# Twelve half quarters of two down projections as seven block products each, in a fused two-block kernel on one core

## The chip, the cores and the metric

One NeuronCore of a Trainium2 chip runs the whole program. The metric is the device time of one execution in microseconds (us); a shorter time is better. TensorE (PE in the profile) multiplies matrices into the eight PSUM banks, VectorE (DVE), ScalarE (ACT) and GpSimd (POOL) work on elements, and SyncE (SP) issues transfers.

## The reference

Two transformer blocks run one after the other on 512 tokens of width 1024. Each ends with a feed-forward network, and only these two networks are changed:

```python
hf = _rmsnorm(h, norm_ffn_g[l]) @ w_ff1[l]                # first block, 1024 -> 4096
h = h + jnp.square(jax.nn.relu(hf)) @ w_ff2[l]            # 4096 -> 1024
...
m = rmsnorm(x, norm_pre_mlp[l])                           # second block
y = jnp.square(jax.nn.relu(m @ w_up[l])) @ w_down[l]
x = x + rmsnorm(y, norm_post_mlp[l])
```

All is float32. The kernel computes each product from two float32r parts of each operand, the rounded value (`_hi`) and the remainder (`_lo`): hi·hi + hi·lo + lo·hi, three matmuls for one.

## The kernel before

The activations lie by feature: 128 features on the partitions, 512 tokens along the row. The weights come as a stream of chunks of 128x1024 elements (512 KB), in the order of use, through a ring of four buffers. For each chunk SP issues the load into `w_raw` (L386 to L389), ACT rounds it to `w_hi` (`round_chunk`, L1213 to L1218, three chunks ahead), POOL subtracts to give `w_lo` (`remainder`, L408 to L410), and PE does `chunk` (L524): eight blocks of the inner dimension, three matmuls for each (`three`, L511, through `mm`, L509), all into one bank. A chunk is 24 matmuls of 128x128 weights on 512 columns.

A feed-forward network (`feed_forward`, at L826 on PE, L1500 on ACT, L2161 on DVE) is four quarters (`FF_GROUPS = 4`), and a quarter is eight up chunks and then eight down chunks. Behind each up chunk DVE takes relu(bank)·rstd into `ff_t` (L2146), ACT squares it into `ff_f` (L1494) and rounds that to `b_hi` (L1496), and DVE makes `b_lo` (L2149). Behind each down chunk DVE adds the bank to `res` or `ffy` (L2157; L2154 copies it for the first quarter of the second network). The first network is the stage FF1, the second FF2. The first up chunks of each run beside the end of the stage before: in FF1 chunks 0 and 1 take turns block by block while the residual is being split, in FF2 chunks 0 to 2 run by halves of the tokens while POOL and DVE finish the residual (`post_add`, L481 to L485). Each engine takes its instructions in the written order, so a wait on a semaphore holds all that stands behind it on that engine.

Of the kernel before, what the change touches and what calls it, by code (L numbers as in the profile page):

```python
# [20 lines left out]
ALU = mybir.AluOpType  # L21
ACT = mybir.ActivationFunctionType
AX = mybir.AxisListType
F32 = mybir.dt.float32
# [3 lines left out]
P = 128  # L28
# [22 lines left out]
FF_GROUPS = 4  # L51
# [10 lines left out]
          ("GL", 3), ("AO", 8), ("CO", 8), ("MX", 8), ("QX", 4), ("OX", 4), ("FF1", 64), ("CQ", 2), ("CKV", 1),  # L62
          ("KR", 1), ("QK", 4), ("UQ", 2), ("UKV", 1), ("OA", 1), ("VM", 4), ("OM", 3), ("WO", 8), ("FF2", 64)]
CH = {}
_n = 0
for _name, _count in STAGES:
# [5 lines left out]
        ("GL", 3), ("AO", 8), ("CO", 8), ("MX", 8), ("QX", 4), ("OX", 8), ("FF1", 64), ("CQ", 2), ("CKV", 1),  # L72
        ("KR", 1), ("QK", 4), ("UQ", 8), ("UKV", 8), ("OA", 1), ("VM", 4), ("OM", 3), ("WO", 11), ("FF2", 68)]
# [94 lines left out]
def program(nc, stream, xT, memT, cols_in, consts_in, pos_in, out):  # L168
    with ExitStack() as ctx:
# [80 lines left out]
        ff_f = at("ff_f", [P, 2, T], TMP0 + 4096)  # L250
# [68 lines left out]
        x_landed = [sem(f"x_landed{i}") for i in range(RING)]  # L319
# [43 lines left out]
        def up_bank(s, g, o0, j):  # L363

            if s == 1 and g == 0 and j in (4, 5):
                return j + 2
            return (o0 + j) % RING
# [6 lines left out]
        def _(sp):  # L374
# [11 lines left out]
            with sp.Fori(1, CHUNKS // RING) as i:  # L386
                for j in range(RING):
                    sp.wait_ge(chunk_done, RING * i + j - (RING - 1))
                    sp.dma_start(w_raw[:, j, :],  # L389
                                 stream[bass.ds(RING * i + j, 1), :, :].rearrange("o p n -> (o p) n")  # L390
                                 ).then_inc(raw_landed[j], 16)
            vector_adds = [j for j in range(KB) if j not in POOL_ADDS]
# [12 lines left out]
        def _(pool):  # L405
# [6 lines left out]

            last = CH["FF2"] // RING
# [7 lines left out]
            pool.wait_ge(sems["first_hi"], 1)  # L421
            first_remainder(0, sems["first_lo"])
# [3 lines left out]
            with pool.Fori(1, CH["CQ"] // RING) as i:  # L426
                for j in range(RING):
                    remainder(RING * i + j, j)
            pool.wait_ge(sems["pv_done"], 4 * MLA_G)
# [65 lines left out]
            with pool.Fori(last + 1, CHUNKS // RING) as i:  # L495
                for j in range(RING):
                    remainder(RING * i + j, j)
# [9 lines left out]
        def _(pe):  # L507
# [147 lines left out]
            def first_values():  # L655
                for kk in range(2):
                    w = slice(kk * T, (kk + 1) * T)
                    pe.wait_ge(w_hi_done if kk else sems["first_hi"], 1)
# [3 lines left out]
                for kk in range(2):  # L662
                    w = slice(kk * T, (kk + 1) * T)
                    pe.wait_ge(w_lo_done if kk else sems["first_lo"], 1)
# [161 lines left out]
            def feed_forward(name, s, hset, norm, norm_at, upto=2 * KB, done=0):  # L826
                c0, o0 = CH[name], O[name]

                def ff_chunk(g, j, ready=None, base=0, ks=range(KB)):
                    hi, lo = (a_hi, a_lo) if j < KB else (b_hi, b_lo)  # L830
                    if isinstance(g, int) and up_bank(s, g, o0, j) >= RING:
                        chunk(c0 + j, (c0 + j) % RING, None, up_bank(s, g, o0, j), hi, lo)
                        return
                    chunk(g * 16 + (c0 + j), (c0 + j) % RING, g * 16 + (o0 + j), (o0 + j) % RING, hi, lo, T,
                          ready, base, first=o0 + j, ks=ks)

                if not done:
                    for k in range(KB):
                        ff_chunk(0, 0, sems["hg_ready"], KB * hset, range(k, k + 1))
                        ff_chunk(0, 1, ks=range(k, k + 1))  # L840
                    done = 2
                ff_chunk(0, done, ks=range(norm_at))
                norm()
                ff_chunk(0, done, ks=range(norm_at, KB))
                for j in range(done + 1, 2 * KB):
                    ff_chunk(0, j, sems["f_ready"] if j == KB else None, 32 * s)
                with pe.Fori(1, FF_GROUPS - 1) as g:
                    for j in range(2 * KB):
                        ff_chunk(g, j, sems["f_ready"] if j == KB else None, g * KB + 32 * s)
# [1940 lines left out]
```

## Time and profile before

| | |
|---|---|
| time, three runs | 1583.17 us median (1582.39 to 1584.31) |
| profiled execution, first to last instruction | 1579.8 us span |
| PE busy | 1545.0 us, 98% of the span |
| DVE, ACT, POOL busy | 838.6, 652.4, 653.6 us |
| largest share of the chain that ended last | PE, 90% |

The profile is one execution. Its span leaves out what lies before the first and behind the last instruction: 3.4 us to the median of the runs. Matmuls overlap in the pipeline, so the spacing of their starts tells their cost, not the duration of one.

### The profile page before, as it was taken

What the parts mean: (1) busy time and instruction counts of PE and PEld (TensorE: products, weight loads), DVE (VectorE), ACT (ScalarE), POOL (GpSimd) and SP (SyncE); (2) the same over time, 40 slices, a digit from 0 to 9 for tenths busy, and PEclk for the clock granted to TensorE, in tenths of its full rate; (3) what the DMA queues carried; (4) which work ended last, traced back from release to release, by engine and by line L of the source; (5) the groups of instructions that cost most, each with busy time, mean ns of one, the idle gap of its engine ahead of it and who ended that gap; (6) DMA issues with size and microseconds to landing.
All of it is one profiled execution on the core that took longest, in us unless ns stands there. A gap on an engine that the chain in (4) does not pass through costs nothing.

```text
span 1579.8 us, 21097 instructions
## 1 busy us (share of the span) xinstructions
PE 1545.0 (98%) x7370; PEld 1278.8 (81%) x7370; DVE 838.6 (53%) x1486; ACT 652.4 (41%) x1066; POOL 653.6 (41%) x299
## 2 busy tenths in 40 slices
PE   8999999999999999999999999999999999999997
PEld 6888888787788877888888888777778888888887
DVE  5689999877785446442112124877645612111125
ACT  6553333444552445523233244455754514232331
POOL 3454444323344433444444445442524544444442
PEclk9999999999999999999999999999999999999999
DMA  5332333222333322323333333221112333333332
GB/s 208 102 121 94 94 101 98 67 67 67 107 95 102 96 67 67 101 93 99 101 93 93 104 96 94 83 71 61 41 49 73 96 104 93 94 98 102 94 93 81
DMA packets 41412, 144.57 MB, mean 92 GB/s; under 512 B 4596, under 2 KB 6772, under 8 KB 41080
## 3 DMA queue, kind: packets, MB, share of 16 engines
q1 hardware_dynamic: 40320, 139.94, 28.7%
q10 hardware_dynamic: 1016, 3.62, 0.7%
q8 instruction: 48, 0.79, 0.2%
q14 instruction: 28, 0.23, 0.1%
HBM read 141.43 MB, written 2.11 MB: 91 GB/s over the span
## 4 chain that ended last, share of the span: by engine, by line
PE 90%; DVE 4%; issue 3%; ACT 2%; POOL 1%; DMA 0%; DVEq 0%; SPq 0%; POOLq 0%; ACTq 0%
PE bank L509 88%; PE bank L619 1%; POOL w_lo L410 1%; POOL res L485 1%; DVE cq_rstd L1767 0%; PE bank L1014 0%; DVE bias L1913 0%; ACT w_hi L1218 0%; DMA x_raw<-in_xT 0%; DMA w_raw<-in_stream 0%; ACT kT L1392 0%; DVE cn_lo L2261 0%; DVE gt L2284 0%; DVE ffy L2600 0%; ACT probs L1251 0%
## 5 line engine op out<-in xcount | busy, mean ns | idle before, releaser
L410 POOL TENSOR_TENSOR w_lo<-w_raw,w_hi 128x1024 fp32r<-128x1024 f32 x250 | 602.6, 2411 | 849.6 <-ACT w_hi L1218 849.2
L1218 ACT CAST w_hi<-w_raw 128x1024 fp32r<-128x1024 f32 x255 | 267.4, 1049 | 499.2 <-DMA w_raw<-in_stream 499.2
L509 PE MATMUL bank<-a_hi,w_hi 128*128 128x512 f32 (+1 forms) x1120 | 445.0, 397 | 3.1 <-DVE a_lo L2520 1.8
L509 PE MATMUL bank<-a_hi,w_lo 128*128 128x512 f32 (+1 forms) x1120 | 431.5, 385 | 0.0
L509 PE MATMUL bank<-a_lo,w_hi 128*128 128x512 f32 (+1 forms) x1120 | 431.2, 385 | 0.0
L509 PEld LDWEIGHTS bank<-a_hi,w_hi 128*128 128x128 f32 x1120 | 210.5, 188 | 50.9 <-issue 4.2
L509 PEld LDWEIGHTS bank<-a_lo,w_hi 128*128 128x128 f32 x1120 | 210.6, 188 | 45.6 <-issue 3.6
L509 PEld LDWEIGHTS bank<-a_hi,w_lo 128*128 128x128 f32 x1120 | 210.4, 188 | 42.3
L509 PE MATMUL bank<-b_hi,w_hi 128*128 128x512 f32 (+1 forms) x640 | 244.3, 382 | 0.0
L509 PE MATMUL bank<-b_hi,w_lo 128*128 128x512 f32 (+1 forms) x640 | 242.3, 379 | 0.0
L509 PE MATMUL bank<-b_lo,w_hi 128*128 128x512 f32 (+1 forms) x640 | 242.2, 378 | 0.0
L509 PEld LDWEIGHTS bank<-b_hi,w_hi 128*128 128x128 f32 x640 | 120.4, 188 | 22.8 <-issue 0.2
L509 PEld LDWEIGHTS bank<-b_lo,w_hi 128*128 128x128 f32 x640 | 120.4, 188 | 22.5 <-issue 0.2
L509 PEld LDWEIGHTS bank<-b_hi,w_lo 128*128 128x128 f32 x640 | 120.4, 188 | 22.5
L2146 DVE SCALAR_TENSOR_TENSOR ff_t<-bank,rstd 128x512 f32<-128x512 f32 x64 | 44.1, 689 | 148.5 <-PE bank L509 148.4
L2149 DVE TENSOR_TENSOR b_lo<-ff_f,b_hi 128x512 fp32r<-128x512 f32 x64 | 47.9, 748 | 86.8 <-ACT b_hi L1496 86.8
L1977 DVE SCALAR_TENSOR_TENSOR bank<-conv_in,cols,bank 128x512 f32<-128x512 f32 x114 | 82.3, 749 | 1.6
L2157 DVE TENSOR_TENSOR res<-bank,res 128x512 f32<-128x512 f32 x32 | 22.1, 691 | 109.0 <-PE bank L509 109.0
L1956 DVE SCALAR_TENSOR_TENSOR bank<-conv_in,cols,bank 128x512 f32<-128x512 f32 x116 | 76.5, 745 | 0.0
L1494 ACT ACTIVATE ff_f<-ff_t 128x512 f32<-128x512 f32 x64 | 40.5, 632 | 85.5 <-DVE ff_t L2146 85.5
L2157 DVE TENSOR_TENSOR ffy<-bank,ffy 128x512 f32<-128x512 f32 x20 | 13.8, 691 | 84.3 <-PE bank L509 84.3
L1260 ACT COPY probsT<-bank 128x256 f32<-128x256 f32 (+3 forms) x48 | 19.6, 409 | 58.0 <-PE bank L619 58.0
(355 smaller groups left out, 1961.3 us busy)
## 6 DMA issues: line engine op xcount, KB each, us to landing
w_raw<-in_stream SPq DMA_DIRECT2D x255, 512.0 KB, 3.5
res<-in_xT ACTq DMA_DIRECT2D x1, 2048.0 KB, 8.0
out_y<-y_out SPq DMA_DIRECT2D x16, 128.0 KB, 1.8
x_raw<-in_xT SPq DMA_DIRECT2D x3, 512.0 KB, 8.3
mem_raw<-in_memT SPq DMA_DIRECT2D x1, 1024.0 KB, 11.9
mrow<-m_rows ACTq DMA_DIRECT2D x4, 256.0 KB, 3.2
w_raw<-in_stream SPq DMA_DIRECT2D x2, 256.0 KB, 3.6
x_raw<-in_xT SPq DMA_DIRECT2D x2, 256.0 KB, 4.2
```

Of the source, the lines that this page charges most:

```text
L410: nc.gpsimd.tensor_tensor(w_lo[:, j, :], w_raw[:, j, :], w_hi[:, j, :].bitcast(F32), ALU.subtract).then_inc(w_lo_done, 1)
L485: nc.gpsimd.tensor_tensor(res[:, j, t], res[:, j, t], mixed[:, j, t], ALU.add).then_inc(sems["post_added"], 1)
L509: return nc.tensor.matmul(o, l, r, start=start, stop=stop)
L619: m = nc.tensor.transpose(turned_bank(U)[:, r], probs[:, U % 2, r], ident)
L1218: A.copy(w_hi[:, slot, :], w_raw[:, slot, :]).then_inc(w_hi_done, 1)
L1260: A.copy(probsT[:, U % 2, r], turned_bank(U)[:, r]).then_inc(sems["pT_copied"], 1)
L1494: A.activation(ff_f[:, j % 2, :], ff_t[:, j % 2, :], ACT.Square).then_inc(sems["f_sq"], 1)
L1956: V.scalar_tensor_tensor(out=blk(conv_io, e, 0, T) if last else acc, in0=u, scalar=w, in1=acc, op0=ALU.mult, op1=ALU.add).then_inc(sems["c ...
L1977: m = V.scalar_tensor_tensor(out=out, in0=u, scalar=w, in1=acc if start is None else start, op0=ALU.mult, op1=ALU.add)
L2146: V.scalar_tensor_tensor(out=ff_t[:, j % 2, :], in0=bank, scalar=0.0, in1=rstd[:, :], op0=ALU.max, op1=ALU.mult).then_inc(evac_dve, 1)
L2149: V.tensor_tensor(b_lo[:, j, :], ff_f[:, j % 2, :], b_hi[:, j, :].bitcast(F32), ALU.subtract).then_inc(sems["f_ready"], 1)
L2157: V.tensor_tensor(dst[:, i, :], bank, dst[:, i, :], ALU.add).then_inc(evac_dve, 1)
```

## The change

Of each network's 32 blocks of inner dimension, 24 are now done in six "half quarters" of four blocks (`HALVES = 6`), and the last quarter (eight blocks) as before. A half quarter is four up chunks (`ff_up`) and then a product of 512 tokens x 512 inner x 1024 outputs, cut in two along each dimension and done by seven products of half size (Winograd's form of Strassen's scheme) instead of eight. Blocks 0 and 2 of a half quarter are the "even" ones, 1 and 3 the "odd" ones.

- PE (`product`, `ff_down`): seven products M1, M5, M7, M6, M4, M2, M3, each 12 matmuls of 128 tokens as the weights and 512 outputs as the columns, so 84 instead of 96. Results lie by token in `ytok`. At the end `turn_block` turns them back, four transposes for each of eight blocks of outputs.
- POOL (`left_sum`, `rest`): four sums of 128x1024 weight pieces in each half quarter (S3, S1, S2, S4), and seven remainders `dn_rest` instead of four. `dn_rest` lies on `dn_raw`, so a piece is loaded again only when its product is done (`left` on SP).
- ACT (`top`): seven roundings of weight pieces instead of four, the squares, and the roundings of seven combinations of the activations.
- DVE: relu alone (`evict_up`; the factor rstd², `r2`, now comes at the very end), four sums of activations for each pair of blocks and five subtractions for `f7_lo` (`even_block`, `even_lo`, `odd_block`), 14 additions of banks (`take`), once per network seven additions of 128x1024 or so (`ff_whole`), and `add_turned`.
- The loops of these stages on PE, SP, ACT, DVE and POOL are written out.

```diff
@@ SP @@
+            def left(s, g, which):
+                for name, last in zip(LEFT, (M1, M5, M4, M2)):
...
+                    if g > 0:
+                        sp.wait_ge(sems["dn_done"], done_before(s, g - 1) + 2 * (last + 1))
...
+                    sp.dma_start(dn_raw[:, SLOT[name], :], stream[CHUNKS + 4 * q + LEFT.index(name)]
@@ POOL @@
+            def left_sum(s, g, name):
+                if name == "S3":
+                    landed("L11")
+                    landed("L21")
...
+                    ins = nc.gpsimd.tensor_tensor(slot("S3"), slot("L11"), slot("L21"), ALU.subtract)
+                elif name == "S1":
+                    landed("L22")
...
+            def rest(s, g, names=BY_ORDER):
+                for name in names:
+                    if name == "L11":
+                        left_sum(s, g, "S3")
+                        left_sum(s, g, "S1")
+                        left_sum(s, g, "S2")
+                    elif name == "S2":
+                        left_sum(s, g, "S4")
...
+                    nc.gpsimd.tensor_tensor(dn_rest[:, n, :], dn_raw[:, n, :], dn_top[n].bitcast(F32), ALU.subtract
...
+            for g in range(HALVES):
+                rest(0, g)
+                for c in range(CH["FF1"] + 4 * (g + 1), CH["FF1"] + 4 * (g + 2)):
+                    remainder(c, c % RING)
...
+            remainder(CH["FF2"] + 4, 0)
+            rest(1, 0, ("L11",))
+            remainder(CH["FF2"] + 5, 1)
+            rest(1, 0, BY_ORDER[1:])
@@ PE @@
+            def product(s, g, n, x, banks):
+                pe.wait_ge(sems["apart_lo"], APART + PRODUCTS * q + n + 1)
+                for h in range(2):
+                    for p in range(2):
...
+                        mm(o, xh, wh, p == 0, False)
+                        mm(o, xh, wl, False, False)
+                        m = mm(o, xl, wh, False, p == 1)
+            def ff_down(s, g):
...
+                pe.wait_ge(sems["b_ready"], b_at(s, last, 1))
+                product(s, g, M1, E1, (4, 5))
...
+                pe.wait_ge(sems["b_ready"], b_at(s, last, 3))
+                product(s, g, M7, T3, (0, 1))
...
+                pe.wait_ge(sems["dn_evac"], evac + 2 * (M7 + 1))
+                product(s, g, M4, T4, (0, 1))
@@ ACT @@
+            def ff_half(s, g):
+                j = 4 * g
+                square_up(s, j)
+                even_casts(s, j)
+                top(s, g, "S2", "L22")
+                square_up(s, j + 1)
+                odd_casts(s, j + 1)
+                top(s, g, "L12", "S4")
+                square_up(s, j + 2)
+                even_casts(s, j + 2)
+                square_up(s, j + 3)
+                odd_casts(s, j + 3)
+                round_to(ff_chunk_at(s, j + 7) - AHEAD)
...
+            for g in range(1, HALVES):
+                top(0, g, "L11", "S1", "S3")
+                ff_half(0, g)
@@ DVE @@
+            def ff_half(s, g):
+                j = 4 * g
+                evict_up(s, j)
+                even_block(s, j)
+                even_lo(s, j)
+                evict_up(s, j + 1)
+                odd_block(s, j + 1)
+                evict_up(s, j + 2)
+                even_block(s, j + 2)
+                even_lo(s, j + 2)
+                evict_up(s, j + 3)
+                odd_block(s, j + 3)
+                take_products(s, g)
```

On DVE `even_block` is one subtraction of 128x256 (`t1`), `even_lo` two (`E1`, `T1`); `odd_block` is three sums of 128x256 (here c1, c2, c3) and the remainders of `T3` (128x256), `T2` and `T4` together, and `O1` and `O2` together (128x512 each). All nine read two operands in SBUF.

## Rows read from the trace of the kernel before

**Rows 1.** The page: PE's busy time, and the chain that ended last by engine.
```profile
PE 1545.0 (98%) x7370; PEld 1278.8 (81%) x7370; DVE 838.6 (53%) x1486; ACT 652.4 (41%) x1066; POOL 653.6 (41%) x299
PE 90%; DVE 4%; issue 3%; ACT 2%; POOL 1%; DMA 0%; DVEq 0%; SPq 0%; POOLq 0%; ACTq 0%
```

**Rows 2.** Busy time by stretch, one inside FF1, one in FF2 (PE, PEld, DVE, ACT, POOL; clock; DMA).
```profile
700.00:800.00 100.00, 100.00 (x443) 82.81 (x442) 19.57 (x27) 29.62 (x36) 43.88 (x19) 1.00 0.34 100
...
1400.00:1500.00 100.00, 100.00 (x443) 82.84 (x442) 20.05 (x29) 32.04 (x40) 43.22 (x18) 1.00 0.33 98
```

**Rows 3.** Timeline of PE in FF1, first and last of 57 consecutive matmuls (start, duration).
```profile
699.66 0.39 PE L509 MATMUL bank<-b_lo,w_hi 128*128 128x512 f32 x1
...
712.36 0.39 PE L509 MATMUL bank<-b_hi,w_hi 128*128 128x512 f32 x1
```

**Rows 4.** Timelines of DVE and ACT behind one up chunk of FF1.
```profile
753.36 0.69 DVE L2146 SCALAR_TENSOR_TENSOR ff_t<-bank,rstd 128x512 f32<-128x512 f32 x1 [2.71 <-PE bank L509]
755.40 0.69 DVE L2149 TENSOR_TENSOR b_lo<-ff_f,b_hi 128x512 fp32r<-128x512 f32 x1 [1.35 <-ACT b_hi L1496]
...
754.08 0.63 ACT L1494 ACTIVATE ff_f<-ff_t 128x512 f32<-128x512 f32 x1 [1.34 <-DVE ff_t L2146]
754.75 0.62 ACT L1496 CAST b_hi<-ff_f 128x512 fp32r<-128x512 f32 x1
```

**Rows 5.** Timelines of DVE and POOL at two places where they meet.
```profile
19.75 7.09 DVE L1831 TENSOR_TENSOR x_sq<-x_sq 128x512 f32<-128x512 f32 x4
...
20.75 2.73 POOL L410 TENSOR_TENSOR w_lo<-w_raw,w_hi 128x1024 fp32r<-128x1024 f32 x1 [12.92 <-ACT w_hi L1218]
23.70 2.59 POOL L410 TENSOR_TENSOR w_lo<-w_raw,w_hi 128x1024 fp32r<-128x1024 f32 x1 [0.21 <-ACT w_hi L1218]
...
1180.79 2.46 DVE L2089 TENSOR_TENSOR ssq<-ssq,sq 128x512 f32<-128x512 f32 x1 [2.97 <-ACT sq L1451]
...
1180.31 2.40 POOL L410 TENSOR_TENSOR w_lo<-w_raw,w_hi 128x1024 fp32r<-128x1024 f32 x1 [7.68 <-ACT w_hi L1218]
1182.93 2.59 POOL L410 TENSOR_TENSOR w_lo<-w_raw,w_hi 128x1024 fp32r<-128x1024 f32 x1 [0.23 <-ACT w_hi L1218]
```

**Rows 6.** Timelines of POOL's subtractions that follow each other at once; DVE beside the first.
```profile
51.02 5.66 DVE L1867 SCALAR_TENSOR_TENSOR mem_lo<-mem_raw,cols,mem_hi 128x256 fp32r<-128x256 f32 x4 [0.69 <-ACT mem_hi L1328]
...
50.65 4.94 POOL L410 TENSOR_TENSOR w_lo<-w_raw,w_hi 128x1024 fp32r<-128x1024 f32 x2 [5.76 <-ACT w_hi L1218]
...
117.62 4.76 POOL L410 TENSOR_TENSOR w_lo<-w_raw,w_hi 128x1024 fp32r<-128x1024 f32 x2 [2.25 <-ACT w_hi L1218]
...
1237.26 7.25 POOL L410 TENSOR_TENSOR w_lo<-w_raw,w_hi 128x1024 fp32r<-128x1024 f32 x3 [8.17 <-ACT w_hi L1218]
```

**Rows 7.** Groups by line and shape: small DVE and ACT operations, and ACT's rounding.
```profile
L2528 DVE TENSOR_TENSOR mixed<-mixed 128x256 f32<-128x256 f32 x2 | 0.9, 426 | 0.1
...
L1746 ACT ACTIVATE sq<-ffy 128x256 f32<-128x256 f32 x8 | 3.3, 417 | 15.9 <-DVE ffy L2594 15.9
...
L1218 ACT CAST w_hi<-w_raw 128x1024 fp32r<-128x1024 f32 x255 | 267.4, 1049 | 499.2 <-DMA w_raw<-in_stream 499.2
```

**Rows 8.** The page's DMA issues (KB each, median us from issue to landing).
```profile
w_raw<-in_stream SPq DMA_DIRECT2D x255, 512.0 KB, 3.5
```

**Rows 9.** Timeline of PE at the end of FF1's chunks 0 and 1, and of POOL near it.
```profile
638.69 1.02 PE L509 MATMUL bank<-ssq,consts 128*128 128x512 f32 x2
...
635.20 2.40 POOL L410 TENSOR_TENSOR w_lo<-w_raw,w_hi 128x1024 fp32r<-128x1024 f32 x1 [4.05 <-ACT w_hi L1218]
```

**Rows 10.** Timeline of PE where FF2's chunk 4 starts.
```profile
1239.71 0.50 PE L509 MATMUL bank<-a_hi,w_hi 128*128 128x512 f32 x1 [0.32 <-POOL w_lo L410]
```

**Rows 11.** Timeline of PE: four transposes of probabilities (128x128, float32).
```profile
305.89 0.60 PE L619 MATMUL bank<-consts,probs 128*128 128x128 f32 x4
```

**Rows 12.** Timeline of PE's first matmuls.
```profile
5.82 3.88 PE L509 MATMUL bank<-w_hi,xu_hi 128*128 128x512 f32 x8 [5.82 <-ACT xu_hi L1297]
9.54 2.01 PE L509 MATMUL bank<-w_lo,xu_hi 128*128 128x512 f32 x8
```

More of the change, by code:

```diff
@@ L50, with done_before, evac_before, added_at @@
 MLA_V = 64
-FF_GROUPS = 4
+HALVES = 6
+UPS = 4 * HALVES
+BY_ORDER = ("L11", "S1", "S3", "S2", "L22", "L12", "S4")
+SLOT = {name: n for n, name in enumerate(BY_ORDER)}
+LEFT = ("L11", "L21", "L22", "L12")
+SLOT["L21"] = SLOT["S1"]
+M1, M5, M7, M6, M4, M2, M3 = range(7)
+E1, O1, O2, T1, T3, T2, T4 = range(7)
+PRODUCTS = 7
+PARTS_DONE = 2 * PRODUCTS
+WHOLE_STEPS = 7
+def done_before(s, g):
+    return (PARTS_DONE * HALVES + KB) * s + PARTS_DONE * g
+def evac_before(s, g):
+    return (PARTS_DONE * HALVES + WHOLE_STEPS + 1 + 2 * KB) * s + PARTS_DONE * g
+def added_at(s, i):
+    return evac_before(s, HALVES) + WHOLE_STEPS + 1 + (2 - s) * (i + 1)
+def evens_first(s, g):
+    return s == 1 and g < 2
+def b_before(s, g):
+    return (10 * HALVES + KB) * s + 10 * g
+def b_at(s, j, n):
+    g, p = j // 4, j // 2 % 2
+    if evens_first(s, g):
+        return b_before(s, g) + (2 * p + n if n <= 2 else 2 + 3 * p + n)
+    return b_before(s, g) + 5 * p + n
+def sum_at(s, j, n):
+    g, p = j // 4, j // 2 % 2
+    if evens_first(s, g):
+        return 8 * (HALVES * s + g) + (p + n if n == 1 else 1 + 3 * p + n)
+    return 8 * (HALVES * s + g) + 4 * p + n
 RING = 4
@@ L391, in _ @@
                                  ).then_inc(raw_landed[j], 16)
+            for c in range(CH["FF1"] // RING * RING, CH["FF1"]):
+                ring(c)
+            left(0, 0, ("L11", "L21"))
+            ring(CH["FF1"])
+            left(0, 0, ("L22", "L12"))
+            for c in range(CH["FF1"] + 1, CH["FF1"] + 4):
+                ring(c)
+            for g in range(HALVES):
+                if g > 0:
+                    left(0, g, LEFT)
+                for j in range(4):
+                    ring(CH["FF1"] + 4 * (g + 1) + j)
+            for c in range(CH["FF1"] + UPS + 4, CH["FF2"] + 4):
+                ring(c)
+            left(1, 0, LEFT)
+            for c in range(CH["FF2"] + 4, CH["FF2"] + 10):
+                ring(c)
+            left(1, 1, LEFT)
+            for c in range(CH["FF2"] + 10, CH["FF2"] + 12):
+                ring(c)
+            for g in range(2, HALVES):
+                left(1, g, LEFT)
+                for j in range(4):
+                    ring(CH["FF2"] + 4 * (g + 1) + j)
+            for c in range(CH["FF2"] + UPS + 4, CHUNKS):
+                ring(c)
             vector_adds = [j for j in range(KB) if j not in POOL_ADDS]
@@ L494, in _ @@
                 post_add(1, j)
-            with pool.Fori(last + 1, CHUNKS // RING) as i:
-                for j in range(RING):
-                    remainder(RING * i + j, j)
+            remainder(CH["FF2"] + 4, 0)
+            rest(1, 0, ("L11",))
+            remainder(CH["FF2"] + 5, 1)
+            rest(1, 0, BY_ORDER[1:])
+            remainder(CH["FF2"] + 6, 2)
+            remainder(CH["FF2"] + 7, 3)
+            rest(1, 1)
+            for g in range(2, HALVES):
+                for c in range(CH["FF2"] + 4 * g, CH["FF2"] + 4 * g + 4):
+                    remainder(c, c % RING)
+                rest(1, g)
+            for c in range(CH["FF2"] + UPS, CHUNKS):
+                remainder(c, c % RING)
             for h in range(2):
@@ L823, in _ @@
                 m.then_inc(chunk_done, 1)
[L826 to L849, printed above, removed]
-                g = FF_GROUPS - 1
-                for j in range(upto):
-                    ff_chunk(g, j, sems["f_ready"] if j == KB else None, g * KB + 32 * s)
@@ L2587, in end_out @@
                 j, a, b = PARTS[n]
[L2588 removed]
+                o = O["FF2"] + UPS + KB + n
                 if n < KB:
@@ L2729, in _stream @@
     assert len(chunks) == CHUNKS
-    return np.stack(chunks)
+    return np.stack(chunks + halved)
 def _packed(i):
```

543 lines of the change are left out of this document (427 added, 116 removed).

## Prediction, made before the changed kernel was run

> **What bounds the kernel now.** I read the page first: PE is busy for 1545.0 of 1579.8 us and carries 90% of the chain that ended last [rows 1]. Then the stretches: inside both feed-forward networks PE has no idle time, while DVE is busy for some 20% and POOL for 44% [rows 2]. The timeline gives what a matmul costs: 56 steps from 699.66 to 712.36, 0.2268 us each, at a granted clock of 1.00 [rows 2, 3]. So each matmul saved in these stages is worth 0.227 us, as long as the other engines keep up. The rest of the argument is whether they do.
>
> **What is saved on PE.** 12 half quarters x 12 matmuls x 0.2268 = 32.7 us. One half quarter costs PE 4 x 24 + 96 = 192 matmuls, 43.5 us, before, and 96 + 84 = 180, 40.8 us, after: 21.8 for the up chunks and 19.0 for the products.
>
> **What is added on PE.** 64 transposes of 128x128. Four of them take 0.60 us in all [rows 11], so 0.15 each at most, and 0.11 if the pipeline's tail of the last is left out: 7 to 9.6 us, I take 8. The Trainium skill, page "TensorE: Matmul & The Clock Gate", section "Part 4: PE-mode transpose", gives about 275 ns in a kernel's context; by it this term would be 17.6 us. The trace disagrees, at 0.15 or less.
>
> **How POOL and DVE meet.** This decides the case. In the change POOL has 15 operations of 128x1024 in each half quarter (4 `w_lo`, 4 sums, 7 remainders), and DVE 18 with both inputs in SBUF (14 of 128x256, 4 of 128x512). POOL's take 2.38 to 2.42 us, also one behind the other (4.76 for two, 7.25 for three [rows 6]). The sums aren't in the trace; they have the same shape and number of inputs, so I take 2.4. That makes 36 us in 40.8: POOL alone fits, with 5 us over.
>
> But the two engines don't run such operations side by side. At 1180.79 DVE begins a 128x512 addition that takes 2.46 us; POOL's subtraction had begun at 1180.31 and ends at 1182.71, and DVE ends 0.54 later. Alone such an operation takes 0.69 [rows 4]. The next of POOL, which is waiting by then, shows 2.59 instead of 2.4 and ends 2.81 behind its predecessor: it stood behind DVE's. The other place shows who comes next. DVE has four such operations in line at 19.75 and needs 7.09 us for them, and POOL's two (20.75 to 23.48, 23.70 to 26.29) lie between them one for one [rows 5]. In the second pair of POOL, beside four DVE operations of 128x256, POOL's two take 4.94, 0.2 more than 4.76, so only one of DVE's four got in between, and DVE needs 5.66 us [rows 6]. So: while POOL has work in line, each two-input DVE operation waits for one whole POOL operation. The Trainium skill, page "SBUF — State Buffer", section "SBUF: two separate sides", names it an exclusive lock on a shared port pair, taken by whichever starts first and held for the whole instruction; by that rule, the trace agrees (2.46 against 0.69). Operations with one input in PSUM (`evict_up`, `take`) aren't touched; those behind a bank are 0.69 [rows 4].
>
> **A half quarter in its steady course**, counted from the start of M1. A 128x256 operation is 0.42 on DVE and at most 0.42 on ACT, a rounding of 128x1024 1.05 [rows 7], a square and a 128x512 rounding 0.63 [rows 4], a load lands 3.5 after its issue [rows 8].
> - PE: M7 may start at 5.4, M4 ends at 13.6, M2 at 16.3, M3 at 19.0, the next up chunks at 24.5, 29.9, 35.4, 40.8.
> - ACT rounds the next four up chunks only behind `odd_casts` of block 3. POOL is idle then, so block 3 goes fast: relu 0.35 to 1.0, square 1.7, c1 to c3 by 3.0, last casting 4.35, first `w_hi` 5.4. M7's `T3` is there at 3.4, so no wait. DVE's 14 additions follow the products and are 9.7 us, hidden.
> - POOL: four `w_lo` 5.4 to 15.0, S3 to 17.4, S1 to 19.9 (L22 can be loaded only when M4 is done: 13.6 + 3.5 and the tail), S2 to 22.3, L11's remainder to 24.8. From here on, up chunk 0 is done, and POOL is in line without a gap.
> - DVE: relu to 25.5, square 26.15; then `t1` waits for POOL until 27.2 and ends at 27.5, `E1` at 30.0, `T1` at 32.6, relu of block 1, c1 at 35.2, c2 at 37.75: five waits for a POOL operation. POOL's next, L12's remainder, needs ACT's `top`, which stands behind `odd_casts` of block 1, and these wait for c3 (38.25). So POOL now idles for 3 us, which it can't give back. `top` of L12 ends at 40.55, of S4 at 41.6. Only behind it stands the square of block 2 (42.25), though its chunk was done at 35.4. `t1` of block 2 waits for L12's remainder (43.05), `E1` for S4's (45.6), and ends at 45.95.
> - M1 needs this `E1`. It starts at 46.0 instead of 40.8: PE stands for 5.2 us.
>
> So 46.0 us against 43.5 before: **+2.5 us** for each half quarter in the steady course. It repeats itself, since POOL's start hangs on block 3, and block 3 on M1. Bounds: with none of the seven waits the same chain gives `E1` of block 2 at 37.8, PE is never held, and the half quarter is 40.8 (-2.7); with each step of the chain 0.1 longer (some 20 steps) it is 48 (+4.5).
>
> **The first half quarters.** FF1's chunks 0 and 1 and a third's first block are 51 matmuls before 638.69, so FF1 starts at 627.1, and POOL's fourth `w_lo` of it runs from 635.20 [rows 9], +8.1. It is followed by the three sums and L11's remainder (to +20.1), and ACT waits for S1 (+15.3) before it takes the root and the first square (+18.3). From there the same chain as above, with DVE held at each step, brings `E1` of block 2 at +41. PE could start M1 at 22.7. The half quarter costs 41 + 19 = 60 instead of 44: **+16**. In FF2, chunk 4 starts at 1239.71 [rows 10], when POOL ends `w_lo` for it; POOL then does three sums and a remainder before the `w_lo` of chunk 5, so that chunk starts at 1252 instead of 1245: 7 us. DVE then has 18 two-input operations for two pairs of blocks against POOL's line, and a reciprocal of 3.35 before `take_products`: M7's banks are taken at 1276, M4 waits 5 us. The second half quarter has only two up chunks before its products and some 31 us of POOL work behind S4's remainder of the first: another 5. About 17 us by the end of the second: **+16.5**. Bounds for these two terms: 7 and 8 if DVE never waits for POOL (what stays are sums in front of `w_lo` and `top` in front of squares), 22 and 24.
>
> **Small terms.** `ff_whole`, seven DVE additions of 8 to 10 us, lies under the last eight up chunks, which need DVE only from the fifth on. The transfers carry the same bytes. The clock: PE's first eight matmuls, after 5.82 us of standing, start over 3.72 us instead of 1.8 [rows 12]. Whether 5.2 us between busy stretches bring that about no row shows; 0 to 1.9 for each of some 13 stalls, 0 to 25 us, I take 6.
>
> **Sum.** FF1 16 + 5 x 2.5 = 28.5; FF2 16.5 + 4 x 2.5 = 26.5; transposes 8; clock 6: +69, so a span of 1579.8 + 69 = 1649. The median lies 3.4 above the span: 1652.
>
> **Rivals.**
> - *DVE doesn't wait.* If the waits are much rarer than I read (POOL's line has gaps at its semaphores, into which DVE fits), PE sets the pace: -32.7 + 8 + 7 + 8 = -10, 1573. For it: POOL has 5 us over, and its operations that wait for its own sums leave gaps of some 0.1. Against: one for one in every place where both had work in line [rows 5, 6]. It decides where fewer than two of the seven waits are left (5.2 us of stall are two waits of 2.4).
> - *Some waits fall away.* If DVE's next operation gets in ahead of POOL half the time, three waits of 2.4 leave M1 on time or 0.5 late: 41 us, -2.3 x 11 = -25, and with 11 + 12 for the starts and 8: 1589. If only one or two fall away: 1600 to 1630.
> - *The clock falls at every stall.* Same course, 25 instead of 6: 1671. Slower matmuls come straight on top, as the chain starts anew with up chunk 0.
> - *The loads or PE's own waits between products cost.* 168 product halves with 0.1 each: 17 us on top where PE sets the pace, nothing where it stands anyway.
>
> **Chances.** Forecast with its clock bounds (1630 to 1675) 0.6; some waits fall away (1580 to 1630) 0.22, of which 0.02 within 0.2% of no change; DVE doesn't wait 0.12; beyond 1675 0.06. Range 1590 to 1680: it holds the forecast, most of the second and part of the last, 0.8. A measurement of this kernel tells 0.2%, some 3 us, from no change. Faster 0.13, same 0.03, slower 0.84.
>
> **What would show it.** Right: in a half quarter of FF1 PE idle for about 5 us before M1, released by DVE's `f7_lo`; two-input 128x256 operations of DVE with a mean far above 0.42, 1.5 to 2 us; POOL at 80% there, with idle time released by ACT's `top`; half quarters 46 us apart. Wrong: PE busy throughout and half quarters 41 apart; or the stall before M7 or M4 instead of M1, which would mean block 3 also meets POOL. The step most open to error is the number of waits in the chain to `E1` of block 2, since one wait more or less is 2.4 us x 10.

## The result, and the profile after

The changed kernel takes 1680.87 us (median of four runs, 1679.59 to 1684.53); the kernel before took 1583.74 on the same chip (1582.39 to 1584.63). The ratio is 1.0618, with a 95% interval of 1.0602 to 1.0634. The profiled execution has a span of 1677.5 us against 1579.8, so 97.7 us have to be found where I had forecast 69. The median is 29 us above the predicted 1652 and 0.9 above the upper end of the range, 1680.

The page of the changed kernel: busy time of the engines, and the chain that ended last by engine.
```profile
PE 1553.0 (93%) x7290; PEld 1278.0 (76%) x7290; DVE 1158.0 (69%) x1814; ACT 704.7 (42%) x1174; POOL 860.1 (51%) x383
PE 81%; DVE 8%; issue 7%; ACT 2%; DMA 1%; POOL 1%; SPq 0%; DVEq 0%; ACTq 0%; POOLq 0%
```
PE's share of the chain fell from 90% to 81% [rows 1], and 7% is "issue", time for which the view names nothing that PE waited for. Its matmuls became fewer and its busy time rose: slower ones are among them.

Busy time by stretch of the changed kernel, as in [rows 2]: inside FF1, and two pieces of 20 us of it.
```profile
720.00:740.00 20.00, 20.00 (x90) 16.55 (x89) 9.73 (x15) 6.29 (x7) 16.88 (x8) 1.00 0.35 106
800.00:820.00 20.00, 15.29 (x60) 12.17 (x59) 15.72 (x22) 11.57 (x17) 11.70 (x5) 0.83 0.30 84
700.00:800.00 100.00, 90.56 (x383) 74.00 (x382) 66.78 (x75) 36.27 (x51) 77.27 (x33) 0.95 0.30 90
```
PE was busy for all of such a stretch before. Now it is for 90.56 of 100, DVE has gone from 19.57 to 66.78, POOL from 43.88 to 77.27, and the granted clock is 0.95. The loss isn't spread: 720 to 740 is as full as before, 800 to 820 holds a hole.

Timelines of the changed kernel around that hole: PE, DVE, ACT, POOL.
```profile
810.62 0.77 PE L694 MATMUL bank<-dn_first,f_hi 128*128 128x512 f32 x1 [4.71 <-issue]
```
```profile
792.49 2.63 DVE L2472 TENSOR_TENSOR f_lo<-ff_f,f_hi 128x256 fp32r<-128x256 f32 x1
795.04 2.61 DVE L2475 TENSOR_TENSOR f_lo<-comb,f_hi 128x256 fp32r<-128x256 f32 x1
797.58 0.68 DVE L2458 TENSOR_SCALAR ff_t<-bank 128x512 f32<-128x512 f32 x1
798.95 1.24 DVE L2484 TENSOR_TENSOR comb<-ff_f 128x256 f32<-128x256 f32 x1 [0.70 <-ACT ff_f L1742]
800.12 2.61 DVE L2485 TENSOR_TENSOR comb<-ff_f,comb 128x256 f32<-128x256 f32 x1
802.76 0.43 DVE L2487 TENSOR_TENSOR comb<-ff_f,comb 128x256 f32<-128x256 f32 x1
...
807.96 2.56 DVE L2472 TENSOR_TENSOR f_lo<-ff_f,f_hi 128x256 fp32r<-128x256 f32 x1
```
```profile
804.27 1.99 ACT L1736 CAST dn_second<-dn_raw 128x1024 fp32r<-128x1024 f32 x2
806.17 0.63 ACT L1742 ACTIVATE ff_f<-ff_t 128x512 f32<-128x512 f32 x1
```
```profile
787.54 7.30 POOL L577 TENSOR_TENSOR dn_rest<-dn_raw,dn_first 128x1024 fp32r<-128x1024 f32 x3
794.80 2.57 POOL L557 TENSOR_TENSOR dn_raw<-dn_raw 128x1024 f32<-128x1024 f32 x1
797.51 2.40 POOL L577 TENSOR_TENSOR dn_rest<-dn_raw,dn_first 128x1024 fp32r<-128x1024 f32 x1
799.88 2.57 POOL L577 TENSOR_TENSOR dn_rest<-dn_raw,dn_second 128x1024 fp32r<-128x1024 f32 x1
805.40 4.84 POOL L577 TENSOR_TENSOR dn_rest<-dn_raw,dn_second 128x1024 fp32r<-128x1024 f32 x2 [2.95 <-ACT dn_second L1736]
```
Read it backwards. M1 starts at 810.62, when DVE's remainder `E1` of block 2 (L2472, 807.96) has ended at 810.52; PE's idle time is put down to "issue", but the operand it needs came at that moment. That remainder is an operation of 128x256 that takes 2.56 us. Such operations have 1.2 to 2.6 us where POOL has a subtraction under way (1.24 at 798.95, which begins when half of POOL's is over), and 0.43 where it hasn't (802.76, in the gap of POOL from 802.45 to 805.40). POOL's gap ends with ACT's rounding of L12, the first of the two that run from 804.27 to 806.26, and the square of block 2 stands behind them at 806.17. It is the forecast chain: ACT's order, POOL's gap, the two remainders, `E1`.

Timeline of PE: matmuls behind the stall of the half quarter before, to where the pace returns.
```profile
762.88 0.77 PE L694 MATMUL bank<-dn_first,f_hi 128*128 128x512 f32 x1 [4.71 <-issue]
763.45 0.63 PE L694 MATMUL bank<-dn_rest,f_hi 128*128 128x512 f32 x1
763.88 0.63 PE L694 MATMUL bank<-dn_first,f_lo 128*128 128x512 f32 x1
...
766.86 0.47 PE L694 MATMUL bank<-dn_first,f_hi 128*128 128x512 f32 x1
767.17 0.39 PE L694 MATMUL bank<-dn_rest,f_hi 128*128 128x512 f32 x1
767.40 0.40 PE L694 MATMUL bank<-dn_first,f_lo 128*128 128x512 f32 x1
```
The stretches before and behind it (PE, PEld, DVE, ACT, POOL; clock; DMA):
```profile
753.00:758.00 5.00, 5.00 (x23) 3.94 (x21) 4.61 (x6) 2.51 (x4) 2.05 (x2) 1.00 0.35 105
763.00:767.00 4.00, 4.00 (x10) 3.13 (x11) 2.91 (x8) 2.37 (x5) 0.00 (x0) 0.50 0.00 0
```
This was the row that I lacked. Before the stall PE had worked at a granted clock of 1.00 (2.4 GHz); then it stood for 4.71 us. Behind the stall the granted clock is 0.50 (1.2 GHz) and the matmuls start 0.43 us apart; after ten of them, 4.29 us, they start 0.23 apart again. Ten at 0.2268 would be 2.27, so 2.0 us come on top of the stall. Behind the other stalls of 4.6 to 4.9 us it is 1.7 to 2.1. The Trainium skill, page "TensorE: Matmul & The Clock Gate", section "Part 1: The HAM clock gate (the "warmup" mystery)", has the clock fall in an idle engine and come back under work; by it, the trace agrees.

**Where 97.7 us come from**, in the terms of the prediction. The idle times ("stalls") are those that PE's timeline shows; a half quarter with a stall s costs s - 2.72 against before, 2.72 being the 12 matmuls that it saves. The last term sums, from 635 on, what the starts of PE's 128x512 matmuls lie apart beyond 0.2268, for those more than 0.26 apart with PE busy in between.

| term | forecast | read from the trace after |
| --- | --- | --- |
| FF1, first half quarter | +16 | stall 17.68: +15.0 |
| FF1, five more | +12.5 | stalls 4.73, 4.71, 4.71, 4.62, 4.71: +9.9 |
| FF2, first and second | +16.5 | 1.01, 5.92, 6.54, 0.46, 3.89: +12.4 |
| FF2, four more | +10 | 11.03, 4.61, 4.59, 4.71: +14.1 |
| transposes | +8 | 64 x 0.11: +7 |
| rotary steps moved | 0 | stalls 0.41 and 4.86: +5.3 |
| slow matmuls ("clock") | +6 | 45.3 for 14.8 before: +30, of it 28 behind the 14 stalls of 3.8 us or more |
| sum | +69 | +94, 4 not assigned |

### The profile page after: what moved, and what is told of

It reads as the page before. It is cut to its first block, busy times and chain, and to the rows that moved or that the text cites. A ratio compares the mean times of both kernels' runs of the same rounds, so it can differ in the third digit from the quotient of the medians.

```text
span 1677.5 us, 20805 instructions
## 1 busy us (share of the span) xinstructions
PE 1553.0 (93%) x7290; PEld 1278.0 (76%) x7290; DVE 1158.0 (69%) x1814; ACT 704.7 (42%) x1174; POOL 860.1 (51%) x383
## 3 DMA queue, kind: packets, MB, share of 16 engines
q1 hardware_dynamic: 40320, 139.94, 26.5%
## 4 chain that ended last, share of the span: by engine, by line
PE 81%; DVE 8%; issue 7%; ACT 2%; DMA 1%; POOL 1%; SPq 0%; DVEq 0%; ACTq 0%; POOLq 0%
PE bank L694 79%; DMA w_raw<-in_stream 1%; PE bank L804 1%; DVE f_lo L2475 1%; DVE x_sq L2153 0%; DVE cq_rstd L2089 0%; PE bank L1249 0%; DVE ropet L2625 0%; ACT w_hi L1466 0%; DVE comb L2485 0%; DVE bias L2235 0%; PE bank L1066 0%; DVE comb L2466 0%; POOL w_lo L524 0%; DVE comb L2484 0%
## 5 line engine op out<-in xcount | busy, mean ns | idle before, releaser
L524 POOL TENSOR_TENSOR w_lo<-w_raw,w_hi 128x1024 fp32r<-128x1024 f32 x202 | 487.0, 2419 | 671.5 <-ACT w_hi L1466 671.2
L694 PE MATMUL bank<-dn_first,f_hi 128*128 128x512 f32 x192 | 86.4, 450 | 77.0 <-issue 66.6
L694 PE MATMUL bank<-dn_rest,f_hi 128*128 128x512 f32 x336 | 139.5, 415 | 0.0
L577 POOL TENSOR_TENSOR dn_rest<-dn_raw,dn_first 128x1024 fp32r<-128x1024 f32 x48 | 117.3, 2462 | 9.3 <-ACT dn_first L1736 6.1
L577 POOL TENSOR_TENSOR dn_rest<-dn_raw,dn_second 128x1024 fp32r<-128x1024 f32 x36 | 88.7, 2480 | 32.3 <-ACT dn_second L1736 32.3
L694 PE MATMUL bank<-b_hi,w_hi 128*128 128x512 f32 (+1 forms) x256 | 96.0, 375 | 5.3 <-DVE b_lo L2583 5.3
L694 PE MATMUL bank<-b_lo,w_hi 128*128 128x512 f32 (+1 forms) x256 | 93.6, 366 | 0.0
L694 PE MATMUL bank<-b_hi,w_lo 128*128 128x512 f32 (+1 forms) x256 | 93.6, 366 | 0.0
L694 PE MATMUL bank<-dn_first,f_lo 128*128 128x512 f32 x192 | 83.3, 434 | 0.0
L694 PEld LDWEIGHTS bank<-dn_rest,f_hi 128*128 128x128 f32 x336 | 69.3, 206 | 14.7
```

Of the source, the lines that this page charges most:

```text
L524: nc.gpsimd.tensor_tensor(w_lo[:, j, :], w_raw[:, j, :], w_hi[:, j, :].bitcast(F32), ALU.subtract).then_inc(w_lo_done, 1)
L577: nc.gpsimd.tensor_tensor(dn_rest[:, n, :], dn_raw[:, n, :], dn_top[n].bitcast(F32), ALU.subtract).then_inc(sems["apart_lo"], 1)
L694: return nc.tensor.matmul(o, l, r, start=start, stop=stop)
```

## Experiments

The first question was whether the waits of DVE for POOL are the cause of the stalls at all. All ratios are to the kernel before.

**POOL without reading SBUF.** The eleven operations of POOL in each half quarter (sums and remainders of the down pieces) become memsets of the same place, sized to the same time (512, 1024 and 1024 columns); so the kernel leaves out the products' weight sums and low parts, which are zeros.
```
-   nc.gpsimd.tensor_tensor(slot("S3"), slot("L11"), slot("L21"), ALU.subtract)
+   fill(slot("S3"))      # three memsets, 2.44 us together; so also S1, S2, S4
-   nc.gpsimd.tensor_tensor(dn_rest[:, n, :], dn_raw[:, n, :], dn_top[n].bitcast(F32), ALU.subtract)
+   fill(dn_rest[:, n, :].bitcast(F32))
```


> The changed kernel, but each of GpSimd's eleven operations of a half quarter on weight pieces (four sums, seven remainders) is replaced by memsets of the same place, of 512, 1024 and 1024 elements, one behind the other, some 2.4 us in all if they go at the pace of the 32x4096 memset of before (3.5 us). So GpSimd is busy as long, and all semaphores stay, but it reads nothing from SBUF; the sums and remainders of the products' weights are left out (zeros). Theory of the port: VectorE's operations with two inputs in SBUF wait only for GpSimd operations that read SBUF. Then its 128x256 subtractions behind these memsets take 0.42 us, the stall of 4.7 us before M1 goes, with it the slow matmuls behind it (2.05 us), and ten half quarters fall from 47.7 to about 41, the first ones lose half of their stalls: 1680.9 - 67 - 15 = about 1600 us. Rival: not the port but GpSimd's sums and remainders come too late as data (the chain of semaphores through them sets M1): then, at the same GpSimd time, the stalls stay and the time is 1670 to 1685.

Measured: 1590.92 us, ratio 1.0051 (1.0034 to 1.0067), 9 below what the theory gave and far from the rival's 1670. By line and shape, and by stretch:
```profile
L2480 DVE TENSOR_TENSOR f_lo<-ff_f,f_hi 128x256 fp32r<-128x256 f32 x24 | 10.2, 424 | 0.7 <-ACT f_hi L1757 0.5
```
```profile
700.00:800.00 100.00, 100.00 (x443) 82.85 (x442) 51.46 (x91) 42.55 (x59) 87.33 (x86) 1.00 0.33 106
```
In the changed kernel the first group has this row:
```profile
L2472 DVE TENSOR_TENSOR f_lo<-ff_f,f_hi 128x256 fp32r<-128x256 f32 x24 | 60.1, 2504 | 0.0
```
POOL is even busier (87.33 for 77.27; 28.5 of it are the `w_lo` subtractions, which are unchanged), and DVE's operation takes 0.424 us instead of 2.504. PE is full again. So it isn't POOL's load as such, nor ACT's order by itself, that makes the steady stalls; it is the conflict of two reading engines. 90 us of the 98 go with it. What is left are stalls of 8.17 at FF1's start, 1.03 and 6.24 in FF2's first half quarter, 2.24 in its third and 5.28 at FF1's end, with 11 us of slow matmuls, and so even this kernel is a little slower than before: these use up what the products save.

**ACT's rounding of L12 and S4 behind block 2.** One part of the chain alone.
```
    odd_casts(s, j + 1)
-   top(s, g, "L12", "S4")
    square_up(s, j + 2)
    even_casts(s, j + 2)
+   top(s, g, "L12", "S4")
```


> In the changed kernel's half quarters with four up chunks, ScalarE rounds L12 and S4 behind square and castings of block 2 instead of before them. Theory: the stall before M1 has two parts, ScalarE's 2.0 us of rounding ahead of the square of block 2, and two waits of VectorE for GpSimd's remainders of L12 and S4, which that rounding sets free. Moved back, M1 starts some 3.2 us sooner; but the two remainders then fall into block 3's sums, T3 comes later than M7 wants it (1.5 us), GpSimd's next line starts later by up to 4 us and meets more of VectorE's operations. By hand between 1640 and 1665, with idle time before M7 as well as M1. Rival: ScalarE's order is not on the path, GpSimd's line alone sets the pace: within 0.3% of 1681.

Measured: 1656.84 us, ratio 1.0462 (1.0444 to 1.0479), inside the expected 1640 to 1665. The steady stalls before M1 are 1.9 to 2.9 instead of 4.7; new ones of 1.3 stand before M7 in two half quarters. As the forecast chain says, the rounding in front of the square is worth about 2 us of the stall. It is so only while the port holds DVE: with the memsets and the old order there was no stall.

**Matmuls in place of the pause.** Twenty matmuls that nobody reads stand in front of the wait for M1 in nine half quarters, all but FF1's first and FF2's first two.
```
+   if g > s:
+       for _ in range(20):
+           mm(ps[4][:, :], a_hi[:, 0, 0:P], a_hi[:, 0, :])
    pe.wait_ge(sems["b_ready"], b_at(s, last, 1))
```


> In the nine half quarters with the steady stall, TensorE does 20 more matmuls of 128x512 into bank 4 ahead of the wait for M1 (4.5 us of the 4.7; their result is overwritten). Nothing else is touched. Theory: the ten matmuls at 0.43 us behind each stall are the clock, which falls because TensorE stands; with the stall filled they go at 0.227, the granted clock stays at 1.00 there, and 9 x 2.05 = 18 us are saved: 1662. Rival: the pace behind the stall comes from something else (weights, port, the first wait of a product): the pace stays and the time is 1680 or a little more.

Measured: 1664.58 us, ratio 1.0516 (1.0498 to 1.0533), 16.3 less than the changed kernel (1662 expected). PE's timeline at the same place:
```profile
756.48 4.70 PE L694 MATMUL bank<-a_hi 128*128 128x512 f32 x20
761.33 0.50 PE L694 MATMUL bank<-dn_first,f_hi 128*128 128x512 f32 x1 [0.15 <-DVE f_lo L2475]
761.67 0.40 PE L694 MATMUL bank<-dn_rest,f_hi 128*128 128x512 f32 x1
```
M1 still waits for DVE, but PE has worked until 0.15 us before it, its granted clock stays at 1.00, and it goes on at 0.23 us a matmul from the second on. 180 matmuls more made the kernel faster, so the 2 us behind a stall are the clock's and not the operands'.

**The rotary steps back** beside the last down chunks.
```
-   if j == 4:
+   if j == KB:
        dve.wait_ge(sems["late_landed"], 16)
...
-   if 4 < j < 7:
+   if KB < j < KB + 3:
```


> The rotary tables' VectorE and ScalarE steps are put back beside the last eight down chunks of the first network (from beside its last up chunks 4 to 6), as before the change. Theory: beside the up chunks they and the turned blocks' additions hold VectorE, so that the last b_lo comes 5.3 us late and the first down chunk waits, with slow matmuls behind it; put back, 5.3 + 1.5 to 2 us are saved: 1674. Rival: the turned blocks' additions alone are the delay: 1679 to 1682.

Measured: 1676.89 us, ratio 1.0592 (1.0574 to 1.061), 4.0 less, between the expected 1674 and the rival's 1679. The stalls of 0.41 and 4.86 are gone and one of 2.16 comes later, at 1025.71, behind the down chunks beside which the steps now stand. What they did is seen in DVE's timeline of the changed kernel:
```profile
975.89 0.43 DVE L2629 TENSOR_SCALAR ropet<-ropet 128x512 f32<-128x512 f32 x1
976.23 0.69 DVE L2578 SCALAR_TENSOR_TENSOR ff_t<-bank,rstd 128x512 f32<-128x512 f32 x1
...
979.60 2.56 DVE L2566 TENSOR_TENSOR res<-res,y_part 128x512 f32<-128x512 f32 x1
982.09 0.68 DVE L2578 SCALAR_TENSOR_TENSOR ff_t<-bank,rstd 128x512 f32<-128x512 f32 x1
984.11 0.69 DVE L2583 TENSOR_TENSOR b_lo<-ff_f,b_hi 128x512 fp32r<-128x512 f32 x1 [1.34 <-ACT b_hi L1790]
```
The relu of the last up chunk (982.09) stands behind the steps and `add_turned`, one of whose additions meets POOL (979.60), and `b_lo` of the last chunk is done at 984.80. PE, which waits for it, starts at 984.85.

**Smaller pieces of POOL's work.** If a DVE operation waits for the one POOL operation that holds the port, the wait must shrink with that operation. POOL's eleven are each issued as two of 512 columns, and as four of 256.
```
+   def in_pieces(dst, a, b, op, done):
+       for k in range(2):             # 4 in the other kernel
+           w = slice(512 * k, 512 * k + 512)
+           nc.gpsimd.tensor_tensor(dst[:, w], a[:, w], b[:, w], op).then_inc(done, 1)
```


> GpSimd's eleven 128x1024 operations of a half quarter (four sums, seven remainders) are each issued as two of 128x512; the work is the same. Theory (a two-input VectorE operation waits for the one GpSimd operation that has the port, 2.1 us of its 2.6): a piece is 1.2 us, so the waits of the seven operations before the first product fall from about 2.1 to about 1, some 7 us per half quarter; the 4.7 us stall before the first product goes, and with it its slow matmuls. 1681 less nine or ten stalls of 6.8: about 1620, 1605 to 1640. Rival (GpSimd keeps the port for its whole queue, or each more operation costs it a handover): 1675 to 1700.

> The same eleven operations as four of 128x256 each. Theory: a wait is at most 0.65 us now, so the steady stalls are gone already with halves and what is left are the stalls of the first half quarters; 1600 to 1625, 0 to 10 below the kernel with halves. Rival: GpSimd pays an overhead of 0.1 to 0.2 us per operation, 33 more of them are 3 to 6 us per half quarter, its line becomes late and the time goes up again, 1640 or more.

Measured: halves 1658.41 us, ratio 1.048 (1.0462 to 1.0497), above the expected range; quarters 1647.14, ratio 1.0412 (1.0394 to 1.0429), above it too. DVE's group with halves, then with quarters, and POOL's with quarters:
```profile
L2476 DVE TENSOR_TENSOR f_lo<-ff_f,f_hi 128x256 fp32r<-128x256 f32 x24 | 35.9, 1498 | 0.0
```
```profile
L2476 DVE TENSOR_TENSOR f_lo<-ff_f,f_hi 128x256 fp32r<-128x256 f32 x24 | 22.2, 927 | 0.5 <-ACT f_hi L1753 0.5
L530 POOL TENSOR_TENSOR dn_rest<-dn_raw,dn_first 128x256 fp32r<-128x256 f32 x192 | 157.3, 853 | 3.4
```
The mean goes 2.504, 1.498, 0.927 over the 0.42 of the free port: waits of 2.08, 1.07 and 0.50 us for whole, half and quarter. The wait shrinks with POOL's operation, as the one-for-one rule has it. But my sum for halves was wrong by 38 us. DVE's 128x512 operations (L2496, L2499 with halves) now meet POOL as well, 1.24 and 1.23 us in the mean for 0.78 and 0.77 in the changed kernel. More turns are taken, each cheaper. The steady stalls only fell from 4.7 to between 3.3 and 4.0, and to between 1.7 and 3.1.

With quarters the expectation's rival, that each piece has a price of its own and POOL's line becomes late, came true: it gave 1640 or more. Four pieces behind each other with DVE idle beside them, and three half quarters of FF1 by stretch:
```profile
746.89 2.83 POOL L530 TENSOR_TENSOR dn_raw<-dn_raw 128x256 f32<-128x256 f32 x4
```
```profile
700.00:840.00 140.00, 132.46 (x569) 107.06 (x567) 87.61 (x112) 55.08 (x79) 138.13 (x151) 0.99 0.31 94
```
The four take 2.83 us where a whole takes 2.40, so eleven cut operations cost POOL some 4.7 us more in a half quarter, nearly the 5 us that it had over. It is busy for 138.13 of 140 us and waits for nobody, so almost every two-input operation of DVE finds it at work.

**The sums by VectorE** instead of by GpSimd, from the second half quarter of each network on. They lie between the evictions of the half quarter before; the fourth stands behind block 0's remainders.
```
    take(s, g, M4, y21, (0, 1))
+   sum_of(s, g + 1, "S3")             # V.tensor_tensor(slot S3, slot L11, slot L21, subtract)
    take(s, g, M2, y11, (4, 5))
+   sum_of(s, g + 1, "S1")
+   sum_of(s, g + 1, "S2")
```


> The four sums of each half quarter but the first of each network are made by VectorE between its evictions, not by GpSimd: the change without its last part. GpSimd then has seven remainders and four of the up chunks (26.8 us of 47 for 36.4 + S). Theory: fewer of the seven VectorE operations meet a GpSimd operation; the stall of 4.7 us before the first product goes at most half quarters, VectorE's four operations of 1.2 to 3 us lie in its idle time beside the products: 1625 to 1650. Rival (it is ScalarE's order and VectorE's own line, not GpSimd's load): 1675 to 1695, VectorE being 5 to 10 us longer per half quarter.

Measured: 1645.16 us, ratio 1.0398 (1.0381 to 1.0416), 36 less than the changed kernel, with stalls of 1.7 to 2.0 before M1 in the steady course. A sum of 128x1024 takes DVE 1.350 us in the mean, POOL 2.4, and on DVE it lies in idle time. So of the three parts taken back one by one, this is worth most: 36 us, against 24 for ACT's order and 4 for the rotary steps.

**Reliefs together.** Quarters, the late rounding, the rotary steps back, and in FF1's first half quarter S1 and S3 rounded behind block 0's casts:

> GpSimd's operations in quarters, ScalarE's rounding of L12 and S4 behind the casts of the third block, the rotary steps back beside the last down chunks, and in FF1's first half quarter S1 and S3 rounded behind the first block's casts. Theory, if the stalls' shares simply fall away: 10 to 15 us below the kernel with quarters alone, 1590 to 1610; to be faster than the kernel before (1583) the two stalls at FF2's start would have to go as well. Rival: the parts overlap and it is the same as quarters alone.

Measured: 1634.4 us, ratio 1.0325 (1.0307 to 1.0342): 12.7 below quarters alone, as expected, but outside 1590 to 1610, which started from a time for quarters that was itself too low. Then with the sums on VectorE, the roundings of the first half quarter later still, and in FF2 the remainder of chunk 5 in front of the first sums:

> All the reliefs together: GpSimd's remainders in quarters, the sums from the second half quarter of each network on made by VectorE, L12 and S4 rounded behind the third block's casts, the rotary steps back, in FF1's first half quarter the roundings of S1, S3, S2, L22 behind the second block's casts, and in FF2's start the remainder of chunk 5 ahead of the first sums. Theory (the loss is the waits at the port and the stalls that they make): the steady stalls of 2.3 and 0.9 us with their slow matmuls go (nine to ten times 3 to 4 us), FF1's first from 8 to about 3, FF2's first from 10 to about 5: 1634 less 40 to 45, so 1590 to 1600. Rival (the seven products keep a floor of their own, the reliefs overlap): 1605 to 1630. Faster than before (1583) only if FF2's start goes entirely as well.

Measured: 1602.69 us, ratio 1.0124 (1.0101 to 1.0147), 2.7 above the expected range. A stretch inside FF1:
```profile
720.00:820.00 100.00, 99.92 (x441) 82.37 (x440) 80.28 (x95) 40.87 (x57) 80.76 (x78) 1.00 0.33 100
```
From the third half quarter of FF1 to its end PE no longer stands, the clock is 1.00, and half quarters follow each other by 40.8 us. The forecast for PE alone holds once DVE comes in time. The stalls over 1 us in the half quarters are 3.88, 3.02 and 2.85 in FF1's first two, 5.64, 1.57, 1.32, 3.30 and 3.04 in FF2's first three, and there is 2.52 at the rotary steps: 27 us, and slow matmuls are 14 more.

**Fillers in that kernel**, twelve unread matmuls before M1 in every half quarter.

> The same with twelve matmuls that nobody reads ahead of the wait for the first product in every half quarter, so that TensorE does not pause there. They cost 12 x 12 x 0.227 = 33 us where no wait is left to hide them, and give back at most the slow matmuls where one is. If the steady stalls are gone in the kernel without them, this is 20 to 33 us slower than it; if they are still 2 to 3 us each, the two are equal within 10.

Measured: 1619.65 us, ratio 1.0229 (1.0209 to 1.0249), 17 slower than without them, a little less than the expected 20 to 33. Here there is hardly a pause left to fill.

**Two roundings and the reciprocal later** in that kernel.

> All the reliefs together, and two more in the first half quarters: L12 and S4 are rounded behind the fourth block's casts, and FF1's reciprocal of the norm (3.34 us of VectorE) is made behind the evictions of the second product instead of behind all seven. Theory: the stalls of 3.0 and 2.9 us in FF1's first and second half quarters go, with some slow matmuls: 1590 to 1598, still above the kernel before, because FF2's start (stalls of 5.6, 1.6, 1.3, 3.3 and 3.0) isn't touched. Rival: the fourth block's lateness moves to the sixth and seventh products (S4, L12 rounded later) and it is the same, 1600 to 1606.

Measured: 1598.91 us, ratio 1.0105 (1.0088 to 1.0121), 3.8 below the one with the reliefs together, just above the expected 1590 to 1598. The stall of 3.0 went to 1.2, that of 2.9 became one of 5.1, and the third half quarter of FF2 lost its 3.0. None of these kernels beats the kernel before.

## Why the prediction was wrong, and what of it held

The direction and the course of the steady half quarter came as forecast; the time didn't, and the step that failed is the size of the clock's term, 6 us forecast and 30 measured. It makes 24 of the 29 us by which the time was missed.

- **PE's saving and the transposes.** 40.8 us for a half quarter was seen where nothing holds PE. Transposes start 0.11 us apart; the row below has eight in 1.03 us, the pipeline's tail of the last included. The term of 8 measures 7.
```profile
949.89 1.03 PE L1066 MATMUL bank<-consts,ytok 128*128 128x128 f32 x8
```
- **The steady half quarter** was right in its mechanism and near in its size: the stall is before M1, 4.6 to 4.7 us where I had 5.2, and POOL is at 77% (80%). DVE's seven groups of 128x256 have means of 2.50, 1.69, 1.51, 1.23, 0.90, 0.68 and 0.51 us, 1.29 over all, below the 1.5 to 2 that I had given as a sign: I had taken a full POOL operation for each wait, and several of DVE's begin when POOL's is half over. The memsets show that the port is the cause. The half quarters are 47.6 us apart and not 46, for the reason two points below.
- **The starts.** FF1's first measures +15.0 for +16. FF2's first two measure +12.4 for +16.5, but what I had counted as over at the end of the second was handed to the third: its stall is 11.03, where I had the steady 2.5 over before. POOL's timeline of the changed kernel there, and ACT's:
```profile
1360.70 7.13 POOL L577 TENSOR_TENSOR dn_rest<-dn_raw,dn_second 128x1024 fp32r<-128x1024 f32 x3 [3.28 <-ACT dn_second L1736]
1367.78 9.49 POOL L524 TENSOR_TENSOR w_lo<-w_raw,w_hi 128x1024 fp32r<-128x1024 f32 x4
1377.20 2.43 POOL L542 TENSOR_TENSOR dn_raw<-dn_raw 128x1024 f32<-128x1024 f32 x1
```
```profile
1382.20 2.00 ACT L1736 CAST dn_first<-dn_raw 128x1024 fp32r<-128x1024 f32 x2 [14.93 <-POOL dn_raw L546]
1384.10 0.63 ACT L1742 ACTIVATE ff_f<-ff_t 128x512 f32<-128x512 f32 x1
```
  POOL still has remainders of the second half quarter until 1367.83, its first sum of the third comes at 1377.20, and ACT's rounding of S1 and S3, for which it stood 14.93 us, is in front of block 0's square. Start and steady part of FF2 together still come to 26.5, the forecast sum, but by two errors that cancel.
- **The step that failed is the clock's term**, "0 to 1.9 for each of some 13 stalls ... I take 6". Measured +30: there are 14 stalls of 3.8 us or more, and behind each lie 1.6 to 2.7 us of slow matmuls, behind the longest (17.68) no more than behind the others. The price of one was near my upper bound (25 in all, and a rival at 1671 that takes it); to take a quarter of that bound was wrong, and I had no row for that choice. My only row of slow matmuls was from the kernel's start [rows 12], and the profile gives the granted clock there (5.80 to 9.50) as 1.00, so it didn't show the clock at all. The filler shows that the term is the clock and that it is caused by the pause. Shorter pauses aren't surely priced so: in the kernel with the sums on VectorE, of nine pauses of 1.7 to 2.0 us four have 1.6 to 1.7 us of slow matmuls behind them, at a granted clock of 0.50, and five have 0.1.
- **The rotary steps at nothing** was a second wrong term, 5.3 us and its slow matmuls. It was put at nothing without a reason: the prediction doesn't name these steps. They stand on DVE in the very stretch where relu, `b_lo` and `add_turned` of the last up chunks must follow each other; put back, they cost 4.0 less.
- **The rival "DVE doesn't wait"** was worked out at 1573. With the port free the kernel takes 1590.92; of the 18 us between, some 11 are slow matmuls and 5.3 the rotary steps, the same two terms.
- **Open.** Some 4 of the 97.7 us, and some 6 of the 23 in the kernel with the reliefs together. And why, with halves, DVE and POOL still meet so often: there POOL is busy for 86% of the stretch from 700 to 840, with quarters for 99%.

## What to carry to other kernels

Work that fits an engine by its sum can still be the bound, if it shares a port with an engine that works in a chain: count how many operations of the chain meet it and price each meeting with one whole operation of the other, so long operations of GpSimd that read SBUF beside short dependent ones of VectorE are an expensive pairing. Shorter pieces make a meeting cheaper, but count what each piece costs by itself. Where a saving on TensorE is bought with pauses of a few microseconds, price each pause with the slow matmuls behind it (here 4.7 + 2.0), and look for such a row ahead of the sum. Of a step that is "only moved", name the chain that it now stands in.

## What the runs showed of the hardware

- A memset of GpSimd doesn't hold up VectorE: 0.42 us for 128x256 in the kernel with memsets (some 59 of 100 us of GpSimd's time, and its other subtractions 28.5), 2.5 with subtractions throughout. The Trainium skill, page "SBUF — State Buffer", section "SBUF: two separate sides", says that a VectorE operation with two SBUF inputs is blocked only by a GpSimd one that reads SBUF; the runs agree. A memset of 128x1024 takes GpSimd 0.955 us, a subtraction 2.4.
- One for one isn't without exceptions. In the kernel with the reliefs together VectorE's sum of 128x1024, 1.22 us alone, once took 8.79, while GpSimd had four subtractions of 2.4 in line. Timelines of VectorE and GpSimd:
```profile
1326.39 8.79 DVE L2533 TENSOR_TENSOR dn_raw<-dn_raw 128x1024 f32<-128x1024 f32 x1
```
```profile
1324.62 9.48 POOL L524 TENSOR_TENSOR w_lo<-w_raw,w_hi 128x1024 fp32r<-128x1024 f32 x4
```
  GpSimd's four show no hold at all (9.48 for 9.6), so VectorE was passed over three times. In seven of the nine other half quarters of that kernel such a sum takes 3.0 to 3.1 at the same place. What decides this I can't say.
- Operations of GpSimd have a price of their own. With no VectorE work beside them, its float32 subtractions and sums of 128x512 start 1.25 us apart and those of 128x256 0.70 (medians of 18 and 89 in the kernels with halves and quarters), for 2.40 of 128x1024.
